# The delta recurrence's inverse in 32x32 blocks, with half-size projection steps between

## The reference

```python
h = rms_norm(x, norm_gain[layer])
proj = h @ w_in[layer]                       # q_a, k_a, v_a, z_a, q_i, ..., qkv_b, z_b, beta, a, gates
...
kb = k * beta[..., None]
lower = jnp.where(strict, jnp.einsum('bhnid,bhnjd->bhnij', kb, k) * decay, 0.0)
tmat = jnp.eye(CHUNK) + lower
u = triangular_solve(tmat, v * beta)         # lower, unit diagonal
w = triangular_solve(tmat, kb * jnp.exp(gc))
```

## Time and profile before

| | |
|---|---|
| median of 3 runs | 2482.61 us (2481.43 to 2485.97) |
| profiled execution | 2481.67 us |
| its span | 2479.8 us |
| granted TensorE clock | 0.993 of 2.4 GHz |
| PE busy with matmuls | 2421.1 us, 98% |
| PE loading weights | 1411.0 us, 57% (beside the matmuls) |
| DVE, ACT, POOL busy | 678.4, 465.0 and 135.8 us |

### The profile page before, as it was taken

The page is one execution under the profiler, slowest core; times in us unless marked ns, Lnnn a source line. Parts: engine busy times, 40 slices in busy tenths (PEclk is TensorE's granted clock), DMA queues, the critical chain, the costliest instruction groups (busy, mean ns, idle before and its releaser), DMA issues. The chain is left out here.

```text
span 2479.8 us, 49135 instructions
## 1 busy us (share of the span) xinstructions
PE 2421.1 (98%) x22371; PEld 1411.0 (57%) x22371; DVE 678.4 (27%) x1393; ACT 465.0 (19%) x789; POOL 135.8 (5%) x333
## 2 busy tenths in 40 slices
PE   9999999999999989999999889999999999999999
PEld 8766557856655665888445665344443534353444
DVE  3534542443552553111014542001010101011002
ACT  1522321432232442000014541000000000000001
POOL 5011000011000310000001300000000000000000
PEclk9999999999999999999999999999999999999999
DMA  7522333432235522444436316999999999999992
GB/s 242 159 86 70 102 119 126 146 109 69 86 111 146 171 68 92 156 150 155 152 122 167 129 46 238 392 401 383 393 396 377 369 391 393 408 376 389 397 373 96
DMA packets 194437, 542.42 MB, mean 219 GB/s; under 512 B 29200, under 2 KB 61360, under 8 KB 194224
## 3 DMA queue, kind: packets, MB, share of 16 engines
q1 hardware_dynamic: 180576, 536.82, 59.1%
q10 hardware_dynamic: 13344, 1.35, 0.4%
q0 software_dynamic: 304, 1.05, 0.1%
HBM read 538.12 MB, written 1.05 MB: 217 GB/s over the span
## 5 line engine op out<-in xcount | busy, mean ns | idle before, releaser
L407 PE MATMUL psum<-ring,hT 128*128 128x512 f32 (+3 forms) x1120 | 469.8, 571 | 4.4 <-ACT area L829 2.8
L2733 PE MATMUL psum<-ring,mix 128*32 128x448 f32 x4608 | 438.7, 539 | 0.2 <-DVE mix L2995 0.2
L407 PEld LDWEIGHTS psum<-ring,hT 128*128 128x128 f32 x1120 | 207.0, 190 | 214.3 <-issue 190.5
L2733 PEld LDWEIGHTS psum<-ring,mix 128*32 128x32 f32 x4608 | 148.8, 110 | 282.6 <-issue 280.8
L2348 PE MATMUL psum<-hT,ring 128*128 128x256 f32 x896 | 193.7, 379 | 0.0
L2348 PEld LDWEIGHTS psum<-hT,ring 128*128 128x128 f32 x896 | 170.1, 190 | 23.0
L710 PE MATMUL psum<-hT,ring 128*128 128x256 f32 x768 | 166.4, 379 | 0.0
L710 PEld LDWEIGHTS psum<-hT,ring 128*128 128x128 f32 x768 | 145.9, 190 | 20.7 <-issue 1.0
L2984 DVE TENSOR_TENSOR area<-area,psum 128x1344 f32<-128x1344 f32 x16 | 24.6, 1535 | 457.5 <-PE psum L2733 457.5
L2746 PE MATMUL psum<-area 128*32 128x256 f32 x2688 | 148.2, 379 | 0.9 <-DVE area L2986 0.9
L2733 PE MATMUL psum<-area,mix 128*32 128x448 f32 x1536 | 147.2, 539 | 0.0
(11 more groups left out here) (528 smaller groups left out, 2283.8 us busy)
## 6 DMA issues: line engine op xcount, KB each, us to landing
ring<-in_w_in_dram SPq DMA_DIRECT2D x88, 1024.0 KB, 5.1
ring<-in_moe_w_gate_dram SPq DMA_DIRECT2D x96, 896.0 KB, 7.5
ring<-in_moe_w_up_dram SPq DMA_DIRECT2D x96, 896.0 KB, 8.1
area<-in_moe_w_down_dram SPq DMA_DIRECT2D x112, 512.0 KB, 6.0
ring<-in_moe_w_down_dram SPq DMA_DIRECT2D x112, 512.0 KB, 6.4
area<-in_moe_w_gate_dram SPq DMA_DIRECT2D x32, 896.0 KB, 7.6
area<-in_moe_w_up_dram SPq DMA_DIRECT2D x32, 896.0 KB, 7.0
ring<-in_w_out_dram SPq DMA_DIRECT2D x16, 1024.0 KB, 5.0
```

The lines of the kernel that those rows point to most:

```text
L407: last = nc.tensor.matmul(acc(g)[:, t, 0:d["n"]], lhs(kk, t), w[:, k, :], start=kk == 0, stop=kk == d["nk"] - 1)
L2733: last = nc.tensor.matmul(PS[32 * j:32 * j + 32, 3 * p + b, 0:PIECE].rearrange("p (m n) -> p m n", n=32), tokens(k, b), w[:, :, j, :], sta ...
```

## The change

XI and XT are now kept compact: 32 columns a head and all four diagonal 32x32 blocks on their own 32 partitions, so that a half is 128x128 and not 128x256. Level 0 has one more subtraction (the two 32-column halves of the masked 64-column form are both subtracted from the identity). The transpose is made by VectorE's 32x32 transpose (`turn32`), at level 0 and after each of levels 1 to 4, instead of by PE: L1002, its ScalarE copy and the product L1030 are gone. In levels 1 to 4 PE works on four 32x32 blocks on the diagonal of its array: 16 matmuls a half for V (32 columns) and 16 for the corner (16 columns). Level 5 joins 32x32 blocks: 8 matmuls a half for V, 12 for the corners, which DVE writes straight into XF and into XW, the 64-wide form that level 6 reads. POOL copies the blocks of XI and XT into XW and XF, six copies of 32x128 a half, after level 4, and level 6 waits for them. The projection steps are one matmul each (`fine`), the numbers in GDN_UNITS are doubled, and `spread_tensor` puts at most one of them in a gap, so that one half-size step stands between V and the corner and one behind it.

```diff
@@ gemm_steps
-                        if (k + 1) % max(1, d["per"] // 4) == 0:
+                            if fine and t < T - 1:
+                                yield
+                        if fine or (k + 1) % max(1, d["per"] // 4) == 0:
@@ spread_tensor
-                    for _ in range(min(due - done, 2)):
+                    if done < due:
                         next(other)
@@ layout
-        XI, XT, VV, LM = [square(k) for k in range(4)]
+        XW, XS, VV, LM = [square(k) for k in range(4)]
+        XI, XT, VB = [[v[u].rearrange("p h c -> p (h c)")[:, a:a + P].rearrange("p (h c) -> p h c", h=4) for u in range(2)]
+                      for v, a in ((XS, 0), (XS, P), (VV, 0))]
+        BLOCK32 = [slice(32 * b, 32 * b + 32) for b in range(4)]
+        def block4(b):
+            return PS[:, b, 0:P].rearrange("p (h c) -> p h c", h=4)
-        GDN_UNITS = (4, 7, 8, 9, 10, 11, 12, 13, 14, 15, 16, 17, 20, 23, 24, 25, 26, 27, 28, 29, 30, 32, 32, 32, 32)
+        GDN_UNITS = (8, 14, 16, 18, 20, 22, 24, 26, 28, 30, 32, 34, 40, 46, 48, 50, 52, 54, 56, 58, 60, 64, 64, 64, 64)
@@ gdn_pe, levels 1 to 4
-                            for r in DIAGONAL:
-                                last = nc.tensor.matmul(PS[r, 2 + u, h * 64:h * 64 + 64], LM[u][r, h, :], XT[u][r, h, :],
+                            for b, r in enumerate(BLOCK32):
+                                last = nc.tensor.matmul(block4(2 + u)[r, h, :], LM[u][r, h, BLOCK32[b % 2]], XT[u][r, h, :],
                                                         start=True, stop=True)
...
-                            for r in DIAGONAL:
-                                nc.tensor.matmul(PS[r, 4 + u, h * 32:h * 32 + 32], VV[u][r, h, :],
-                                                 firsts(XI[u], lv)[r, h], start=True, stop=True)
-                        for h in range(4):
-                            for r in DIAGONAL:
-                                last = nc.tensor.matmul(PS[r, 6 + u, h * 32:h * 32 + 32], XI[u][r, h, :],
-                                                        seconds(VV[u], lv)[r, h], start=True, stop=True)
+                            for r in BLOCK32:
+                                last = nc.tensor.matmul(PS[r, 4 + u, h * 16:h * 16 + 16], VB[u][r, h, :],
+                                                        firsts(XI[u], lv)[r, h], start=True, stop=True)
@@ gdn_pe, level 5 (new), between the waits for gdn_X and gdn_V_out
+                        for b in (0, 2):
+                            last = nc.tensor.matmul(block4(2 + u)[BLOCK32[b], h, :], LF[u][BLOCK32[b + 1], h, 0:32],
+                                                    XT[u][BLOCK32[b + 1], h, :], start=True, stop=True)
+                yield "gap"
...
+                        for b in (0, 2):
+                            nc.tensor.matmul(block4(6 + u)[BLOCK32[b], h, :], XI[u][BLOCK32[b], h, :], VB[u][BLOCK32[b], h, :],
+                                             start=True, stop=True)
+                        last = nc.tensor.matmul(block4(4 + u)[BLOCK32[1], h, :], VB[u][BLOCK32[0], h, :], XI[u][BLOCK32[0], h, :],
+                                                start=True, stop=True)
@@ gdn_pe, level 6
+                    pe.wait_ge(sem("gdn_inverse"), 4 * L + 2 * c + u + 1)
@@ gdn_act
+                            ins = nc.scalar.activation(VB[u], block4(2 + u), ACT.Copy)
@@ gdn_pool
-                            s.do(nc.gpsimd.memset(XF[u][HI, :, LO], 0.0))
+                            s.do(nc.gpsimd.memset(XF[u], 0.0))
...
+                    for r in BLOCK32[0:2]:
+                        s.do(nc.gpsimd.tensor_copy(XW[u][r, :, r], XI[u][r]))
+                    for b, r in enumerate(BLOCK32):
+                        ins = nc.gpsimd.tensor_copy(XF[u][r, :, r], XT[u][r])
+        def turn32(u):
+            return nc.vector.transpose(XT[u].rearrange("p h c -> p (h c)"), XI[u].rearrange("p h c -> p (h c)"))
@@ gdn_dve, level 0
+                    s.do(nc.vector.scalar_tensor_tensor(XI[u], XW[u][:, :, 0:32], -1.0, bc(NEAR[:, 5, :].unsqueeze(1), [P, 4, 32]),
+                                                        ALU.mult, ALU.add))
+                    s.do(nc.vector.tensor_tensor(XI[u], XI[u], XW[u][:, :, 32:64], ALU.subtract))
+                    s.after(turn32(u).then_inc(sem("gdn_init"), 1), "gdn_init")
@@ gdn_dve, level 5, then levels 1 to 4
+                            for b in (0, 2):
+                                s.do(nc.vector.tensor_scalar(XF[u][BLOCK32[b], :, BLOCK32[b + 1]], block4(6 + u)[BLOCK32[b]],
+                                                             -1.0, None, ALU.mult))
+                            s.after(nc.vector.tensor_scalar(XW[u][BLOCK32[1], :, 0:32], block4(4 + u)[BLOCK32[1]], -1.0, None, ALU.mult)
+                                    .then_inc(sem("gdn_X"), 1), "gdn_X")
...
-                        s.after(nc.vector.tensor_tensor(xt, xt, z[1], ALU.subtract)
+                        s.after(turn32(u).then_inc(sem("gdn_X"), 1), "gdn_X")
```

More of the change, by code:

```diff
@@ L717, in proj1_pe @@
                     sums(0)
-            for _ in range(4):
+            for _ in range(8):
                 next(p1)
@@ L729, in proj1_pe @@
             sums(1)
-            for _ in range(8):
+            for _ in range(16):
                 next(p1)
@@ L997, in gdn_pe @@
                 yield
-                for u in range(2):
-                    pe.wait_ge(sem("gdn_init"), 4 * L + 2 * c + u + 1)
-                    for h in range(4):
-                        for r in DIAGONAL:
-                            last = nc.tensor.matmul(PS[r, 2 + u, h * 64:h * 64 + 64], XI[u][r, h, :], IDENT[r, r],
-                                                    start=True, stop=True)
-                    last.then_inc(sem("gdn_first"), 1)
                 yield
-                for lv in range(1, LEVELS - 1):
+                for lv in range(1, LEVELS - 2):
                     base = ((2 * L + c) * (LEVELS - 1) + lv - 1) * 2
@@ L1036, in gdn_pe @@
                     pe.wait_ge(sem("gdn_X"), base - 2 + u + 1)
+                    pe.wait_ge(sem("gdn_inverse"), 4 * L + 2 * c + u + 1)
                     for h in range(4):
-                        last = nc.tensor.matmul(PS[LO, 2 + u, h * 64:h * 64 + 64], LC[u][HI, h, :], XT[u][HI, h, :],
+                        last = nc.tensor.matmul(PS[LO, 2 + u, h * 64:h * 64 + 64], LC[u][HI, h, :], XF[u][HI, h, HI],
                                                 start=True, stop=True)
@@ L1044, in gdn_pe @@
                     for h in range(4):
-                        last = nc.tensor.matmul(PS[LO, 4 + u, h * 64:h * 64 + 64], XI[u][LO, h, :], VV[u][LO, h, :],
+                        last = nc.tensor.matmul(PS[LO, 4 + u, h * 64:h * 64 + 64], XW[u][LO, h, :], VV[u][LO, h, :],
                                                 start=True, stop=True)
@@ L1100, in gdn_act @@
                 yield
-                for u in range(2):
-                    s.eng.wait_ge(sem("gdn_first"), 4 * L + 2 * c + u + 1)
-                    s.after(nc.scalar.activation(XT[u], square4(2 + u), ACT.Copy)
-                            .then_inc(sem("gdn_first_out"), 1), "gdn_first_out")
                 yield
@@ L1108, in gdn_act @@
                         s.eng.wait_ge(sem("gdn_V"), ((2 * L + c) * (LEVELS - 1) + lv - 1) * 2 + u + 1)
[L1109 to L1111 removed]
+                        if lv < LEVELS - 1:
+                            ins = nc.scalar.activation(VB[u], block4(2 + u), ACT.Copy)
+                        else:
+                            ins = nc.scalar.activation(VV[u][LO], square4(2 + u)[LO], ACT.Copy)
+                        s.after(ins.then_inc(sem("gdn_V_out"), 1), "gdn_V_out")
                     yield
@@ L1186, in gdn_dve @@
                             continue
-                        z = [PS[:, b + u, 0:128].rearrange("p (g n) -> p g n", n=1 << lv) for b in (4, 6)]
-                        xi, xt = [v.rearrange("p h (b two n) -> p (h b) two n", two=2, n=1 << lv)[:, :, i, :]
-                                  for i, v in enumerate((XI[u], XT[u]))]
-                        s.do(nc.vector.tensor_tensor(xi, xi, z[0], ALU.subtract))
-                        s.after(nc.vector.tensor_tensor(xt, xt, z[1], ALU.subtract)
-                                .then_inc(sem("gdn_X"), 1), "gdn_X")
+                        if lv == LEVELS - 2:
+                            for b in (0, 2):
[3 more added lines that the diff above has]
+                                    .then_inc(sem("gdn_X"), 1), "gdn_X")
+                            continue
+                        z = PS[:, 4 + u, 0:64].rearrange("p (g n) -> p g n", n=1 << lv)
+                        xi = XI[u].rearrange("p h (b two n) -> p (h b) two n", two=2, n=1 << lv)[:, :, 0, :]
+                        s.do(nc.vector.tensor_tensor(xi, xi, z, ALU.subtract))
+                        s.after(turn32(u).then_inc(sem("gdn_X"), 1), "gdn_X")
                     yield
@@ L3395, in _ @@
                 n += 1
```

(2 more changed lines are left out.)

40 lines of the change are left out of this document (19 added, 21 removed).

## The result

The changed kernel takes 2452.08 us (median of four runs, 2448.94 to 2454.80) beside 2483.36 for the kernel before on the same chip (2481.43 to 2485.97): ratio 0.9873, interval 0.9856 to 0.9890. That is 31.3 us less, where 35.5 was forecast; the time lies 5 us above the forecast of 2447, inside the range and inside the forecast's own range. The profiled execution took 2453.92 around its span of 2452.1.

What follows compares the result with a forecast made beforehand. It took TensorE's own list of work, busy 98%, as the bound. Four chunks save 9.2 + 8.6 + 9.2 + 8.5 = 35.5 us, giving 2446.2 or 2447.1; forecast 2447 us, range 2436 to 2465, own range 2438 to 2457.

Steps and rivals of the forecast that it cites:

- Price of a record: PE time for one small matmul record on 32x32 blocks at four positions: 9 ns taken, at most 13.
- Rivals 2 and 3: Small records stay at 29.8 ns, 2493.5 us (chance 0.05); no change, records at 24 to 27 ns, 2478 to 2487 (0.04).
- Rival 2: Handing over a small record limits it, not its block: 29.8 ns as now, 2493.5 us; chance 0.05.
- Half step: A half-size projection step inserted among PE's small matmuls: 0.865 + 0.18 = 1.05 us.
- Clean level: One new level, 1 to 4, on PE without extra waits: 2 x (0.72 + 1.05) = 3.54 us instead of 5.37.
- Level 1: First doubling level, including the wait for ScalarE's L829: 4.07 us in chunk 0, 5.34 in chunk 1.
- Waits for L829: PE idles before level 1's projection step until ScalarE's L829: 0.5 us in chunk 0, 1.8 in chunk 1.
- VectorE's chain: Subtract (0.29 us at most) and transpose (0.33) after Z: X in time at levels 1 to 4, level 5 0.1 late.
- Rope: In chunk 1 after level 3 it holds VectorE 3.0 us, so PE waits 0.7 us.
- Levels 5 and 6: Level 5: 3.82 us at 18 ns a record, plus 0.1 for VectorE; level 6, matmuls kept: 4.34 us.
- Levels 2 to 4: 3 x 3.54 = 10.62: PE time of three new levels in each chunk, 10.62 us, before chunk 1's 0.7 us rope wait.
- Rival 1: PE's clock falls to 1.2 GHz after idle time, up to 1.7 us each; with late X 2454 to 2461; chance 0.16.

Runs made afterwards that it cites:

- e4: Changed kernel with each V matmul of levels 1 to 4 issued twice, same data and result: 2485.43 us, ratio 1.0011.
- e1: Changed kernel with the full-size projection steps of the kernel before, compact blocks and transposes kept: 2459.92 us, ratio 0.9908.
- e6: Changed kernel with a second product on PE instead of VectorE's transpose in levels 1 to 4: 2482.22 us, ratio 1.0005.
- e5: Changed kernel with V matmuls of levels 1 to 4 64 columns wide instead of 32, no more instructions: 2451.88 us, ratio 0.9875.
- e9: Changed kernel with three dummy 256-column matmuls once a layer, in chunk 1 where PE waits for L829: 2450.86 us, ratio 0.9867.
- e3: Changed kernel with a one-column Silu on ScalarE behind chunk 1's last Exp, to load its table early: 2452.53 us.
- e8: Changed kernel with the edits of e7 and e3 together: 2452.94 us, ratio 0.9882.
- e10: Changed kernel with the edits of e7 and e9 together: 2450.86 us, ratio 0.9868.
- e11: e10 with 24 tiny unread matmuls (96 instructions with weight loads) ahead of layer 1's recurrence: 2445.98 us, ratio 0.9852.
- e7: Changed kernel with some projection half steps moved into levels 3 and 4, L829's wait moved to level 2: 2447.69 us, ratio 0.9857.

## Why the prediction was right, and where it was off

- **The bound.** PE's own list, at 98%: right. 31.7 us came off the list in the four stretches and 31.3 off the median.
- **Price of a record.** 9 ns taken, from the earlier trace rows; measured 8.9 for V (64 records in 0.75 less the last one's passage of 0.19) and 8.7 for Z. Rivals 2 and 3 fell with it, and with them the 25 ns of the Trainium skill ("TensorE: Matmul & The Clock Gate", "Wait — 56ns, not 53.3ns?"): 128 records in 1.35 us (e4) don't agree with it. Rival 2's worry, though, "128 instructions have to follow each other in 0.6 us", pointed at the right resource; it looked at a run, where the limit acts on a level.
- **Half step.** 1.05 taken, 1.05 to 1.06 measured. Clean level: 3.54 taken, 3.45 measured (583.74 to 587.19). Level 1: 4.07 and 5.34 taken, 4.01 and 5.29 measured.
- **Waits for L829.** 0.5 and 1.8 taken, 0.49 and 1.77 measured.
- **VectorE's chain.** Transpose 0.33 taken, 0.31 measured; the subtract 0.22, not 0.29. Levels 1 to 5 don't wait for it. Level 6 does: its second V half starts at 172.33, some 0.35 late, behind the last of level 5's corners (L1213, done at 172.27), where 0.1 was charged. e1 shows the half steps as the cover that the text named, with 12.8 us of waits when it is gone.
- **Rope.** 0.7 in each chunk 1 was charged, and there was no such wait. The 3.0 us of the earlier trace rows hold two operations of 0.76 and 0.77 among four of 0.33; in the changed kernel all six take 0.32 or 0.33, from 220.18 to 222.30. That stretched pair was read as a fixed price; what stretched it is not shown.
- **Levels 5 and 6.** 3.92 and 4.34 taken, 3.37 and 4.51 measured (168.14 to 171.51 to 176.02). The 18 ns a record were too dear: Z's 48 records take 0.63 us up to the step, where 1.00 was taken. GpSimd's copies at 0.29 are in time (167.72 to 171.8).
- **The step that failed** is "Levels 2 to 4: 3 x 3.54 = 10.62". The sum took PE's list as the only price and left out what brings the list. Layer 0 shows it: levels 2 to 4 took 11.79 in chunk 0 and 12.07 in chunk 1 at full clock, 1.4 and 1.7 over three times 3.45. Layer 1, chunk 0, lost 2.1 at one border.
- **Rival 1** was half right. The clock fell behind the idle time for L829 in chunk 1 of layer 1, though not in layer 0, and once more behind the new gap. Each fall cost about 1.4 us from start to start, against up to 1.7 in the text.

Account of the stretches, measured 107.06 less foretold 103.2, 3.8: supply +5.3, clock +2.9, rope -1.4, small prices -2.8 (a level 2 to 4 0.09 too dear twelve times, level 5 0.55 too dear and level 6 0.17 too cheap four times, level 1 0.05 too dear four times). The terms add up to 4.0. So the forecast missed two prices of 8.2 us together, and overcharges of 4.2 covered half of them: that the total came out so near is in part luck. The interval of the ratio is 8 us wide, so the total, 31 against 35, tells little by itself; it is the stretches that do.

## What to carry to other kernels

When a change turns few large matmuls into many small ones, count PE's instructions as well as its time: here 256 of them, matmuls and weight loads alike, took 3.45 to 4.12 us in nearly all cases where PE had to wait at both ends, some 15 ns each, whatever they did. Work moved off PE then counts by its instructions (e6), and wider ones cost little (e5, 2.0 us for twice the columns in the recurrence). Gaps named "issue" within a run without waits are read by their place in the instruction stream, and an idle time of 1.8 us in a region of small matmuls may be worth filling (e9).

## What the runs showed of the hardware

- The 65 gaps in the recurrence, in eleven kernels, all stand at the same remainder of 256, and the queue brings one packet of 16 KB for each 256 instructions. All 65 end 1.20 to 1.59 us after their block has landed. From border to border it is 3.45 to 4.12 us in 21 of the 24 cases where both have a gap, and 5.7 to 6.3 in the others.
- The long gaps have a late fetch. In 44 of the 65 cases the fetch of the block started 0.8 to 2.4 us behind the crossing of the border before, in three within 0.3 us of it, and in 18 it started 3.2 to 4.3 behind it; all ten gaps above 1.8 us are among these 18 (in the changed kernel the 1.91 and the 0.95). What decides when a fetch starts remained open.
- The gaps are not the recurrence's alone. Behind it the changed kernel has three (0.93, 1.10 and 2.02 us) and the kernel before two (1.11 and 0.59), at the same remainder of 256.
- Because of it, making PE faster ahead of a border need not help (e3, e8, e10), and where the borders fall is worth as much as a small edit (e11, 4.9 us). Differences of 3 us between variants here are partly that lottery.
- A record of 64 columns on four positions took 14.0 ns (e5), one of 32 columns 8.9 and one of 16 columns 8.7.
- Idle time of about 2 us in such a region brought the clock to 1.2 GHz in some places and not in others: behind 1.91 and 1.76 us in layer 1 of the changed kernel it fell, behind 1.77 in layer 0 it did not, in e7 it fell behind 1.77 in layer 0, and behind 1.98 in layer 1 of e9 it did not. What else decides was not tried.
